# A two-block fp32 network on one core: attention by query tile with both heads at once, ScalarE softmax scaling, real transposes, and a DFT split by output parity

## The chip, the cores and the metric

One core of a Trainium2 chip runs the whole program once. The metric is the device time of that core in microseconds; the median of three runs of the kernel before is 3487.98 us. Engines are named as the profile names them: PE (TensorE, the matmuls), PEld (its weight loads), DVE (VectorE), ACT (ScalarE), POOL (GpSimd) and SP (SyncE, which issues the DMAs).

## What is computed

Two transformer blocks over 512 tokens of width 1024, everything in float32. Cut to the parts that the change touches:

```python
# first block: hybrid_mixer, then memory cross attention, then a mixture of experts
z = h @ w_in                       # aq, ak, av: 8 heads of 64; mu, mv, mo, mi, mf for an mLSTM
y_att = dilated_attention(aq, ak, av)     # causal, three dilated windows, combined by their denominators
y_m   = sigmoid(mo) * (norm(mlstm(...)) + skip * c)
x = x + concat([y_att, y_m]) @ w_out
p = softmax(q @ k.T * Dh**-0.5)           # cross attention: 4 heads, 256 memory keys
x = x + (p @ v) @ w_o

# second block, for each of 2 layers
x = x + 0.5 * swiglu(norm(x), ffn1_w_in[l], ffn1_w_out[l])
q, k, v, uf, ga, gf = split(norm(x) @ mix_w_in[l])
s = q @ k_window.T * Dh**-0.5 + rpb_bias  # neighbourhood attention: 8 rows by 16 columns of an 8 x 64 grid
y_na = softmax(s) @ v_window
y_f  = fft2(uf per group of 128 channels, over (positions, channels)).real
x = x + (sigmoid(ga + b0) * (y_na @ w_na_out) + sigmoid(gf + b1) * (y_f @ w_f_out)) @ w_o
x = x + 0.5 * swiglu(norm(x), ffn2_w_in[l], ffn2_w_out[l])
```

## The kernel before

**Layout.** Activations are feature-major: 128 features on the partitions, 512 tokens along the row. The large products are done in three parts, with each operand split into a high and a low half of type fp32r (`products`, L462 to L464: high x high, low x high, high x low), 8 blocks of 128 features deep, so one call of `gemm` is 24 matmuls of 512 columns. Its weight panel comes by a DMA from SP into `RAW`, ACT rounds it into `WH` (`round_hi`, L855), POOL subtracts (`subtract_lo`, L401) into `WL`, and there are two slots, so a panel is prepared two gemms ahead. DVE takes each result out of `GEMM0`/`GEMM1` (`take`, L1153).

**Order.** All five engines run programs of their own, written by hand; semaphores that count up are the only link. Loops are register loops (`Counts.loop`), and inside one a wait compares a semaphore with a value worked out from the loop register. Stages: memory keys and values; the mixer of the first block, 4 head pairs (a loop of 3 and an unrolled last); output product; cross attention, 2 head pairs, unrolled; router and experts; then a loop over 2 layers with ffn "a", a loop over 4 head pairs ("na"), "comb" and "wo" (gated products), and ffn "b".

**Attention.** One routine on each engine serves the three kinds. It goes through 8 jobs, `jobs = [(h, i) ...]`, first the four query tiles `i` of head 0 of the pair, then those of head 1. For a job PE computes the scores (L533, fp32, 64 rows of the array), DVE adds the bias or the log count (L1180) and reduces the maximum (L1182), ACT takes the exponential and its row sum (L884), DVE inverts the sum (L1188) and multiplies the identity by it (L1189):

```python
chain(v.reciprocal(SMALL[:, 4 + s:5 + s], SMALL[:, 2 + s:3 + s]))
v.tensor_scalar(DIAG[s], IDENT[:, :], SMALL[:, 4 + s:5 + s], None, ALU.mult)
```

PE then transposes and scales in one by an ordinary fp32 matmul with that diagonal (L544), two jobs behind the scores; ACT copies the turned probabilities out of `TURN` into `PT` (L867); and PE multiplies them by the values (L560), three jobs behind the scores, into 64 partitions of `OUT`. An ordinary fp32 matmul stands in the trace as two records, a transpose (`pe.transpose`, L794) as one. Jobs are of 2 key blocks in "na" (192 or 256 keys) and in the cross attention (256 keys), and of 1 to 4 blocks in the mixer.

**The pair in "na".** PE does four gemms (Q, K, V and the Fourier input U), transposes V (L794), does the channel DFT (L801, `CS`: cosine and sine, 256 columns), then the attention with four more gemms (the gates) and the position DFT (L811 and L813: 8 matmuls of 512 columns with `CT` and `NST` into `DEN`) put between its jobs. DVE adds the mask to the two bias tables (L1576) before its first job.

**The mixer pair.** Three gemms, rotation of Q and K (L675, L676), two head products (L683), then the attention with one gemm inside (after the second job's scores), one gemm behind it, and the mLSTM (L692 to L720). ACT does one sigmoid between its exponentials (L902).

## Time and profile before

| | |
|---|---|
| median of 3 runs (lowest, highest) | 3487.98 us (3485.64, 3502.23) |
| profiled execution, span | 3488.2 us |
| PE busy | 3212.4 us (92%), 14634 matmul records |
| DVE busy | 1570.1 us (45%) |
| ACT busy | 773.2 us (22%) |
| POOL busy | 1007.2 us (29%) |
| mean granted TensorE clock | 0.943 |
| mean DMA rate | 94 GB/s |

The profile gives the span from the first to the last instruction of one execution. The profile's page has no other time for that execution; its span lies within the three runs. Busy shares are means over stages with different limits, and a busy PE is not a PE at its peak: the records of consecutive matmuls overlap. A time in the views is the start in us from the beginning of the span, then the duration. PEclk 1.00 is the full clock (2.4 GHz), 0.50 the lower of its two levels (1.2 GHz).

### The profile page before, as it was taken

The numbers are of one execution on the slowest core, as the hardware profiler recorded it, in microseconds if no ns is written. First come the engines' busy times: TensorE is split into PE (matmuls) and PEld (weight loads), VectorE is DVE, ScalarE is ACT, GpSimd is POOL, SyncE is SP. The second block draws the span as 40 slices with busy tenths as digits, with TensorE's granted clock in tenths as the row PEclk, the third lists the DMA queues.
The fourth block names the chain that finished last, engine by engine and source line by source line (L and its number), as shares of the span: only waits on it lengthen the run. The fifth ranks groups of instructions, "written<-read, shape, count | busy, mean of one in ns | idle before, by whom it ended". The sixth has DMA issues, their size and how long they took to land.

```text
span 3488.2 us, 42847 instructions
## 1 busy us (share of the span) xinstructions
PE 3212.4 (92%) x14634; PEld 2520.2 (72%) x14634; DVE 1570.1 (45%) x2036; ACT 773.2 (22%) x1098; POOL 1007.2 (29%) x395
## 2 busy tenths in 40 slices
PE   5888887899999599999998999999999999999997
PEld 4656565678778388877766888888887766678886
DVE  6445575321221542463335642474247333564246
ACT  3233311210100321222223222222222221322121
POOL 2111120100000144442223444444444222344442
PEclk8877887899999799999999999999999999999998
DMA  3110110446646222231212232222222111223232
GB/s 113 43 38 32 38 48 6 160 165 212 210 156 221 97 96 96 96 104 62 68 62 72 85 105 87 96 91 98 94 96 98 63 63 66 66 85 96 97 98 77
DMA packets 87027, 327.43 MB, mean 94 GB/s; under 512 B 9664, under 2 KB 10816, under 8 KB 86336
## 3 DMA queue, kind: packets, MB, share of 16 engines
q1 hardware_dynamic: 86976, 326.76, 28.1%
q8 instruction: 31, 0.51, 0.1%
q14 instruction: 20, 0.16, 0.0%
HBM read 324.63 MB, written 2.10 MB: 94 GB/s over the span
## 4 chain that ended last, share of the span: by engine, by line
issue 56%; PE 26%; POOL 12%; DVE 2%; DMA 1%; POOLq 1%; ACT 1%; DVEq 0%; SPq 0%
POOL WL L401 12%; PE GEMM L462 4%; PE GEMM L463 4%; PE GEMM L464 4%; PE TURN L614 3%; PE SCORE L614 2%; PE GEMM L614 2%; PE GEMM L641 1%; PE DEN L628 1%; DMA E_PANEL<-experts 1%; PE SCORE L600 1%; PE OUT L628 1%; PE TURN L600 1%; POOLq L154 1%; PE TURN L544 1%
## 5 line engine op out<-in xcount | busy, mean ns | idle before, releaser
L401 POOL TENSOR_TENSOR WL<-RAW,WH 128x1024 fp32r<-128x1024 f32 (+1 forms) x379 | 991.5, 2618 | 1866.3 <-ACT WH L855 1866.3
L462 PE MATMUL GEMM<-XH,WH 128*128 128x512 f32 x2152 | 861.0, 400 | 38.6 <-POOL WL L401 32.1
L463 PE MATMUL GEMM<-XL,WH 128*128 128x512 f32 x2152 | 847.9, 394 | 0.0
L464 PE MATMUL GEMM<-XH,WL 128*128 128x512 f32 x2152 | 847.7, 394 | 0.0
L855 ACT CAST WH<-RAW 128x1024 fp32r<-128x1024 f32 (+1 forms) x379 | 416.6, 1103 | 1193.8 <-PE GEMM L464 1178.5
L462 PEld LDWEIGHTS GEMM<-XH,WH 128*128 128x128 f32 x2152 | 410.9, 191 | 149.2 <-issue 52.7
L462 PE MATMUL GEMM<-AH,WH 128*128 128x512 f32 (+1 forms) x1072 | 426.4, 398 | 54.5 <-DVE AL L1164 18.2
L464 PEld LDWEIGHTS GEMM<-XH,WL 128*128 128x128 f32 x2152 | 410.0, 191 | 87.8
L463 PEld LDWEIGHTS GEMM<-XL,WH 128*128 128x128 f32 x2152 | 411.1, 191 | 86.2 <-issue 2.5
L463 PE MATMUL GEMM<-AL,WH 128*128 128x512 f32 (+1 forms) x1072 | 421.4, 393 | 0.0
L464 PE MATMUL GEMM<-AH,WL 128*128 128x512 f32 (+1 forms) x1072 | 421.2, 393 | 0.0
L462 PEld LDWEIGHTS GEMM<-AH,WH 128*128 128x128 f32 x1072 | 206.9, 193 | 110.4 <-issue 24.5
L1163 DVE CAST AH<-PROB 128x512 f32 x104 | 242.2, 2329 | 15.6 <-DVE PROB L1600 2.5
L464 PEld LDWEIGHTS GEMM<-AH,WL 128*128 128x128 f32 x1072 | 206.7, 193 | 42.5
L1153 DVE SCALAR_TENSOR_TENSOR PROB<-GEMM,RS 128x512 f32<-128x512 f32 x88 | 60.9, 692 | 390.8 <-PE GEMM L464 390.8
L463 PEld LDWEIGHTS GEMM<-AL,WH 128*128 128x128 f32 x1072 | 207.2, 193 | 40.7
L1158 DVE SCALAR_TENSOR_TENSOR X<-GEMM,X 128x512 f32 (+1 forms) x96 | 66.4, 692 | 278.9 <-PE GEMM L464 269.1
L417 POOL COPY X<-XN 128x512 f32<-128x512 f32 x4 | 3.5, 885 | 553.8 <-DVE XN L1545 553.8
L544 PEld LDWEIGHTS TURN<-TB,PROB 128*128 128x128 f32 (+1 forms) x480 | 79.6, 229 | 84.6 <-issue 46.2
L544 PE MATMUL TURN<-TB,PROB 128*128 128x128 f32 (+1 forms) x480 | 106.5, 353 | 31.5 <-DVE TB L1189 31.3
L1103 DVE TENSOR_SCALAR XH<-X,VEC (+1 forms) x64 | 126.4, 1976 | 0.0
L897 ACT ACTIVATE TB<-TA 128x512 f32<-128x512 f32 x88 | 55.5, 630 | 260.6 <-DVE TA L1153 260.6
(299 smaller groups left out, 3129.7 us busy)
## 6 DMA issues: line engine op xcount, KB each, us to landing
RAW<-up SPq DMA_DIRECT2D x176, 512.0 KB, 3.3
E_PANEL<-experts SPq DMA_DIRECT2D x128, 512.0 KB, 4.4
RAW<-mix SPq DMA_DIRECT2D x96, 512.0 KB, 3.3
RAW<-down SPq DMA_DIRECT2D x64, 704.0 KB, 4.1
RAW<-experts SPq DMA_DIRECT2D x64, 512.0 KB, 4.4
RAW<-panels SPq DMA_DIRECT2D x43, 512.0 KB, 3.4
AR<-bias SPq DMA_DIRECT2D x16, 320.0 KB, 3.5
X<-xT SPq DMA_DIRECT2D x1, 2048.0 KB, 11.1
```

The lines of the kernel that those rows point to most:

```text
L401: pool.tensor_tensor(WL[slot][:, 0:width], RAW[slot][:, 0:width], f32(WH[slot][:, 0:width]), ALU.subtract).then_inc(split_lo, c.add(split_lo))
L462: pe.matmul(ps, whb, hi, start=(begin and j == 0), stop=False)
L463: pe.matmul(ps, whb, lo, start=False, stop=False)
L464: mm = pe.matmul(ps, wlb, hi, start=False, stop=(end and j == len(blocks) - 1))
L544: mm = pe.matmul(ps[0:size, at * P:(at + 1) * P], PROB[u % 2][:, key - first:key - first + size], DIAG[u % 2], start=True, stop=True)
L600: mm = pe.matmul(bank[:, k * PAIR * P:(k + 1) * PAIR * P], half[:, t * D + d * P:t * D + (d + 1) * P], tile(SEL, t, PAIR * P), start=(t == ...
L614: mm = pe.matmul(ps, tile(E_PANEL[at], k, P), tile(XG, k * PAIR + j, P), start=(k == 0), stop=(k == KD - 1))
L628: mm = pe.matmul(ps[:, :], tile(HID[j], f, P), tile(E_PANEL[at], half), start=(f == 0), stop=(f == FT_MOE - 1))
L855: act.copy(WH[slot][:, 0:width], RAW[slot][:, 0:width]).then_inc(split_hi, c.add(split_hi))
L1103: chain(v.tensor_scalar(hi, x, gain, None, ALU.mult))
L1158: v.scalar_tensor_tensor(x, ps, scale, x, ALU.mult, ALU.add).then_inc(gemm_taken, c.add(gemm_taken))
L1163: chain(v.tensor_copy(hi, src))
```

## The change

- **Jobs.** Attention goes by query tile: the scores of both heads, then the probabilities of both, then the values of both, their matmuls alternating between the heads. There are 4 units instead of 8 jobs. With 2 key blocks the 4 turned blocks of a unit share one `TURN` bank, one copy to `PT` and one signal. `PT` has a new layout, and for the mixer odd units use `TB` and `SQ` for the probabilities.
- **DVE.** One `tensor_tensor_reduce` per head gives minus the logits and their minimum, in place of the sum and the reduction; the built program has it as two instructions, the sum and the reading of its accumulator. One reciprocal serves both heads. The diagonal is gone. The cross attention, which had a plain copy here, now adds a tile of zeros (set once).
- **ACT.** The exponential has scale -1. A new pass per head multiplies the probabilities by the reciprocal (`norms`). In the mixer one weight rounding and the sigmoid move behind the attention.
- **PE.** The transposes are `pe.transpose` with the identity.
- **DFT.** Before the channel DFT, DVE makes the sum and the difference of the two halves of the positions (rows `r` and `r + 4` of the grid) into `SD`; even outputs come from the sum, odd ones from the difference. The position DFT is 8 matmuls of 256 columns. DVE takes its result straight out of `DEN` in a rearranged order.
- **Order in "na".** Written out: three gemms, the first scores, V's transposes, the fourth gemm, and so on. The mask is added to the bias tables before V is taken.
- **Unrolling.** The mixer's loop of 3, the layers and the pairs are Python loops on SP, POOL (layers alone), PE, ACT and DVE; the waits in them compare with constants. The loops inside the ffn, "comb", "wo" and the experts stay. SP waits with a pair's bias DMAs on the scores taken, no longer on the probabilities.

```diff
@@ PE
-            jobs = [(h, i) for h in range(2) for i in range(QT)]
-            def attention(tiles, v, between=None, k_src=KB):
-                for u in range(len(jobs) + 3):
...
-                            mm = pe.matmul(ps[0:size, at * P:(at + 1) * P], PROB[u % 2][:, key - first:key - first + size],
-                                           DIAG[u % 2], start=True, stop=True)
...
+            def turns(tiles, i):
+                first, n = span(tiles[i])
+                blocks = len(tiles[i])
+                together = 2 * blocks <= QT
+                for h in range(2):
+                    pe.wait_ge(probs_ready, c.next(probs_ready))
+                    if h == 0 or not together:
+                        ps, at = turn_bank(), 0
+                    for _, key, size in tiles[i]:
+                        mm = pe.transpose(ps[0:size, at * P:(at + 1) * P], probs(tiles, i, h)[:, key - first:key - first + size], IDENT[:, :])
+                        at += 1
+                    if h == 1 or not together:
                         mm.then_inc(turned_full, c.add(turned_full))
+            def values(tiles, i, v):
+                pe.wait_ge(turned_taken, c.now(turned_taken))
...
+                for n, (at, (place, _, size)) in enumerate(order):
+                    for h in range(2):
+                        from_ = turned_at(tiles)[i][h] + at * P
+                        mm = pe.matmul(OUT[h * HEAD:(h + 1) * HEAD, i * P:(i + 1) * P],
+                                       v[0:size, place * P + h * HEAD:place * P + (h + 1) * HEAD],
+                                       PT[0:size, from_:from_ + P], start=(n == 0), stop=(n == len(order) - 1))
+            def attention(tiles, v, k_src=KB, between=None):
+                scores(tiles, 0, k_src)
+                if between:
+                    between()
+                for i in range(QT):
+                    if i + 1 < QT:
+                        scores(tiles, i + 1, k_src)
+                    if i:
+                        values(tiles, i - 1, v)
+                    turns(tiles, i)
+                values(tiles, QT - 1, v)
...
-                    attention(NEAR, VB, {1: gate, 2: dft, 4: gate, 6: gate, 8: gate})
...
+                    gemm(next_panel(), eight, x_tiles)
+                    scores(NEAR, 1)
+                    turns(NEAR, 0)
+                    pe.wait_ge(halves_ready, c.next(halves_ready))
                     for b in range(2):
                         ps = score_bank()
                         for t in range(2):
                             mm = pe.matmul(ps[:, t * 2 * P:(t + 1) * 2 * P],
-                                           UT[:, (2 * b + t) * P:(2 * b + t + 1) * P], CS[:, :],
+                                           SD[:, (2 * b + t) * P:(2 * b + t + 1) * P], CS[:, :],
                                            start=True, stop=True)
                         mm.then_inc(scores_full, c.add(scores_full))
+                    gemm(next_panel(), eight, x_tiles)
+                    values(NEAR, 0, VB)
+                    scores(NEAR, 2)
+                    turns(NEAR, 1)
...
+                    for b in range(2):
+                        out = DEN[:, b * HALF_T:(b + 1) * HALF_T]
+                        for t in range(2):
+                            at = 2 * b + t
+                            pe.matmul(out, AB[:, at * 2 * P:at * 2 * P + P], tile(CT, at, HALF_T), start=(t == 0), stop=False)
+                            mm = pe.matmul(out, AB[:, at * 2 * P + P:(at + 1) * 2 * P], tile(NST, at, HALF_T),
+                                           start=False, stop=(t == 1))
+                    values(NEAR, 1, VB)
+                    scores(NEAR, 3)
+                    gemm(next_panel(), eight, x_tiles)
+                    turns(NEAR, 2)
+                    gemm(next_panel(), eight, x_tiles)
+                    values(NEAR, 2, VB)
+                    turns(NEAR, 3)
+                    gemm(next_panel(), eight, x_tiles)
+                    values(NEAR, 3, VB)
@@ ACT
+            def norms(tiles, i):
+                act.wait_ge(recips_ready, c.next(recips_ready))
+                for h in range(2):
+                    p = probs(tiles, i, h)
+                    act.activation(p, p, ACT.Copy, scale=stat(2, i, h)).then_inc(probs_ready, c.add(probs_ready))
...
+            def attention(tiles, before=None, between=()):
+                for i in range(QT + 1):
+                    if i < QT:
+                        exps(tiles, i)
+                    if i == 0 and before:
+                        before()
+                    if i:
+                        turned_probs(tiles, i - 1)
+                    if i < QT:
+                        norms(tiles, i)
+                for unit in between:
+                    unit()
@@ DVE
+            def logits(tiles, i, bias):
+                for h in range(2):
+                    p = probs(tiles, i, h)
+                    ps = scores_in()[:, 0:span(tiles[i])[1]]
+                    v.tensor_tensor_reduce(out=p, in0=ps, in1=bias(h, i), scale=-1.0, scalar=-NEG, op0=ALU.add, op1=ALU.min,
+                                           accum_out=stat(0, i, h)).then_inc(scores_taken, c.add(scores_taken))
...
                     take(UT)
+                    v.wait_ge(gemm_taken, c.now(gemm_taken))
+                    near, far = (UT.rearrange("p (c r) -> p c r", r=NA_ROWS)[:, :, r:r + NA_ROWS // 2] for r in (0, NA_ROWS // 2))
+                    for half, op in enumerate((ALU.add, ALU.subtract)):
+                        ins = v.tensor_tensor(tile(SD, half, HALF_T).rearrange("p (c r) -> p c r", r=NA_ROWS // 2), near, far, op)
+                    ins.then_inc(halves_ready, c.add(halves_ready))
@@ all engines
-            with c.loop("mix1", PAIRS - 1):
+            for _ in range(PAIRS - 1):
...
-            with c.loop("layers", LAYERS):
-                with c.loop("na", PAIRS):
+            for l in range(LAYERS):
+                for i in range(PAIRS):
```

Where the instructions stand, in three places. PE in the loop "na" of before, from the end of the position DFT (ISA rows are waits whose value comes from the loop register; `TB` holds the two diagonals):

```order
L540 ISA
L495 ISA
L544 MATMUL TURN<-TB,PROB 64x128
L544 MATMUL TURN<-TB,PROB 128x128
L487 ISA
L533 MATMUL SCORE<-KB,QB 128x192
L540 ISA
L495 ISA
L544 MATMUL TURN<-TB,PROB 128x128 x2
L549 ISA
L556 ISA
L560 MATMUL OUT<-PT,VB 64x128 x2
```

PE in the changed kernel, a pair of "na", between the fourth gemm and the fifth (`BIG` holds `SD` there):

```order
L549 MATMUL SCORE<-KB,QB 128x256 x2
L562 MATMUL TURN<-IDENT,PROB 64x128
L562 MATMUL TURN<-IDENT,PROB 128x128
L562 MATMUL TURN<-IDENT,PROB 64x128
L562 MATMUL TURN<-IDENT,PROB 128x128
L837 MATMUL SCORE<-CS,BIG 128x256 x4
```

The rows of waits are gone, scores come in twos and turns in fours, and the channel DFT stands behind the first unit's turns. On DVE, the changed kernel from the mask to the two halves (`AR` holds the bias tables, `PADU` is U):

```order
L1658 TENSOR_TENSOR AR<-AR 128x640 x2
L1234 SCALAR_TENSOR_TENSOR VT<-GEMM,RS 128x512
L1252 ISA PROB,SMALL<-SCORE,AR 128x192
L1252 ISA SMALL 128x1
L1252 ISA PROB,SMALL<-SCORE,AR 128x192
L1252 ISA SMALL 128x1
L1258 RECIPROCAL SMALL<-SMALL 128x2
L1234 SCALAR_TENSOR_TENSOR PADU<-GEMM,RS 128x512
L1667 TENSOR_TENSOR BIG<-PADU 128x256 x2
```

Before, the two mask additions stood behind U and the copies of the channel DFT, and nothing stood between the taking of U and PE's channel DFT.

## Rows read from the trace of the kernel before

**Rows 1.** The page: busy time by engine, and the granted clock in 40 slices.

```profile
PE 3212.4 (92%) x14634; PEld 2520.2 (72%) x14634; DVE 1570.1 (45%) x2036; ACT 773.2 (22%) x1098; POOL 1007.2 (29%) x395
...
PEclk8877887899999799999999999999999999999998
```

**Rows 2.** Windows: us, busy by engine, PEclk, DMA: mixer, cross, layers' pairs.

```profile
188.32:280.44 92.12, 81.10 (x288) 55.29 (x287) 47.98 (x74) 27.78 (x48) 14.41 (x6) 0.80 0.11 36
...
509.00:543.00 34.00, 31.81 (x104) 21.90 (x104) 12.15 (x36) 7.79 (x24) 0.36 (x1) 0.60 0.04 16
...
1647.47:1719.27 71.80, 69.32 (x302) 50.16 (x301) 24.91 (x49) 16.04 (x34) 19.63 (x8) 1.00 0.21 68
...
2780.15:2855.08 74.93, 72.44 (x302) 52.23 (x301) 24.89 (x50) 16.04 (x35) 19.58 (x8) 0.95 0.19 65
```

**Rows 3.** Timeline, DVE: the pair's first two takes.

```profile
1647.47 0.69 DVE L1153 SCALAR_TENSOR_TENSOR QB<-GEMM,RS 128x512 f32<-128x512 f32 x1 [4.04 <-PE GEMM L464]
1652.91 0.69 DVE L1153 SCALAR_TENSOR_TENSOR KB<-GEMM,RS 128x512 f32<-128x512 f32 x1 [4.75 <-PE GEMM L464]
```

**Rows 4.** Timeline, PE, the same pair: transposes, position DFT, small groups.

```profile
1663.60 0.71 PE L794 MATMUL TURN<-IDENT,VT 128*128 128x128 f32 x5
...
1674.54 1.13 PE L811 MATMUL DEN<-BIG,AR 128*128 128x512 f32 x2
...
1681.60 0.85 PE L544 MATMUL TURN<-TB,PROB 128*64 128x128 f32 x4
...
1684.06 0.71 PE L544 MATMUL TURN<-TB,PROB 128*128 128x128 f32 x4 [1.09 <-DVE TB L1189]
1684.69 0.79 PE L560 MATMUL OUT<-PT,VB 128*64 128x128 f32 x4
1685.42 0.59 PE L533 MATMUL SCORE<-KB,QB 64*128 64x192 f32 x2
```

**Rows 5.** Timeline, PE, 1712.0 to 1712.1: two column halves of the array.

```profile
1712.04 0.27 PE L544 MATMUL TURN<-TB,PROB 128*64 128x128 f32 x1
1712.05 0.27 PE L560 MATMUL OUT<-PT,VB 128*64 128x128 f32 x1
```

**Rows 6.** Waits of PE in the pair 1647.47:1719.27.

```profile
PE TURN L544 <- DVE TB L1189: 1.5, 3, 1.1
```

**Rows 7.** Timeline in the ffn: DVE and POOL at one moment.

```profile
1524.85 3.51 DVE L1103 TENSOR_SCALAR XH<-X,VEC  x1
1524.85 3.22 POOL L401 TENSOR_TENSOR WL<-RAW,WH 128x1408 fp32r<-128x1408 f32 x1 [4.26 <-ACT WH L855]
```

**Rows 8.** Timeline of the pair: POOL at a panel, DVE's mask additions.

```profile
1648.60 2.39 POOL L401 TENSOR_TENSOR WL<-RAW,WH 128x1024 fp32r<-128x1024 f32 x1 [5.65 <-ACT WH L855]
...
1667.29 4.53 DVE L1576 TENSOR_TENSOR AR<-AR 128x640 f32<-128x640 f32 x2
```

**Rows 9.** Waits of PE in the mixer pair 188.32:280.44.

```profile
PE TURN L544 <- DVE TB L1189: 3.3, 3, 1.4
```

**Rows 10.** Timeline, a looped mixer pair, PE: its attention's ends and turns.

```profile
202.53 3.10 PE L533 MATMUL SCORE<-KB,QB 64*128 64x128 f32 x6 [2.75 <-DVE AR L1329]
...
237.46 2.08 PE L544 MATMUL TURN<-TB,PROB 128*128 128x128 f32 x8
...
241.71 0.50 PE L462 MATMUL GEMM<-XH,WH 128*128 128x512 f32 x1
```

**Rows 11.** The unrolled last mixer pair: first scores, and OUT taken by DVE.

```profile
386.13 2.26 PE L533 MATMUL SCORE<-KB,QB 64*128 64x128 f32 x6 [2.46 <-DVE AR L1329]
...
422.71 0.69 DVE L1195 CAST AH<-OUT 128x512 fp32r<-128x512 f32 x1 [5.92 <-PE OUT L560]
```

**Rows 12.** PE groups of the cross attention, 509:577, with idle before.

```profile
L544 PE MATMUL TURN<-TB,PROB 128*128 128x128 f32 x64 | 19.0, 451 | 2.9 <-DVE TB L1189 2.9
...
L462 PE MATMUL GEMM<-AH,WH 128*128 128x512 f32 x5 | 2.7, 542 | 2.8 <-issue 2.8
```

**Rows 13.** DMA queues of the whole program: packets, MB, share.

```profile
q8 instruction: 31, 0.51, 0.1%
```

265 lines of the change are left out of this document (140 added, 125 removed).

## The prediction

> **What bounds the kernel now.** I read the page first: PE is busy in 92% of the span, and the slices where its clock is low are the first seven and a few at the layers' transitions [rows 1]. Then the windows by stage. A mixer pair takes 92.12 us at a mean granted clock of 0.80, a cross attention pair 34.00 us at 0.60, a pair of "na" 71.80 us at 1.00 in the first layer and 74.93 us at 0.95 in the second [rows 2]. In all of them PE works nearly throughout and DVE, ACT and POOL less than 60% of the time, so what PE is given decides, and only waits that PE itself shows count beside it. In "na" those are small: 1.5 us for the diagonals [rows 6], some 2.3 us with the smaller ones. The eight gemms of a pair take 5.44 us each (the distance of two takes, [rows 3]), 43.5 us, and the change leaves them. What is left to change is 71.8 - 43.5 = 28.3 us a pair, 26.0 us of it work of PE: fp32 matmuls of a few blocks. That, eight times, and the attention stretches of the four mixer pairs and two cross pairs are all the change can reach, about 8 x 28 + 4 x 32 + 2 x 27 = 406 us.
>
> **"na", a pair.** *Position DFT.* It runs from 1674.54 to the turn at 1681.60 [rows 4], 7.06 us for 8 matmuls of 512 columns. With 256 columns each: half, **-3.5**. The channel DFT stays at four matmuls.
>
> *Turns.* A group of two turned blocks takes 0.63 us up to the next group (1684.06 to 1684.69), 8 groups are 5.0 us. A real transpose costs (0.71 - 0.27) / 4 = 0.11 us by the five of V, whose one record lasts about 0.27 us [rows 4, 5]. Four groups of four with 0.2 us to start each: 4 x 0.64 = 2.6 us, **-2.4**.
>
> *Values.* A group is 0.73 us (1684.69 to 1685.42, [rows 4]), 8 are 5.8 us. Now a group holds both heads, alternating, each writing its own 64 partitions. If they follow each other, 4 x 1.2 = 4.8; if two matmuls that fill different column halves run at once, 4 x 0.8 = 3.2. The trace has one such pair by chance: a turn of 64 columns and a values matmul of the other head start 0.01 us apart and last 0.27 us each [rows 5]. I take the overlap, **-2.6**; the other end is -1.0.
>
> *Scores.* The two heads use different row halves; before, two jobs that followed each other used the same one. No row shows row halves at once. One scores group takes about 0.5 us up to the gemm behind it, 8 are 4.0 us; at once it is -2.0, one after the other -0.4 (fewer groups). I take **-1.3**.
>
> *Waits.* The wait for the diagonal goes: **-1.5** [rows 6]. The scaling pass on ACT (two of about 0.4 us) lies under a gemm of 5.44 us for units 0, 1 and 3, and for unit 2 between other work; I cost it at nothing, and about 0.5 us a unit if that cover is gone. The tensor_tensor_reduce costs DVE between 0.36 us (the sum alone) and 0.75 us (sum and reduction as now); DVE is at 24.9 of 71.8 us [rows 2] and it is hidden either way.
>
> *A new wait.* PE's channel DFT now waits for the two halves. Behind the fourth gemm PE has the second scores and the first turns, about 1.2 us. DVE has to take U (0.69 us) and make the halves (twice about 0.42 us), about 1.7 us: PE would stand 0.5 us. But ACT rounds a panel at the same release as DVE takes a result, and POOL follows 1.13 us after that take, for 2.39 us [rows 3, 8]. That is while the first half is being made. The trace shows what then happens: POOL and a DVE operation from SBUF to SBUF start at the same 1524.85, POOL takes its 3.22 us and the DVE operation, which alone is under 0.5 us, lasts 3.51 [rows 7]; and the two mask additions, beside two POOL operations, take 4.53 us together [rows 8]. So the second half is ready about 2.4 us later and PE stands 2.9 us. Both ends kept, I take **+2.0**. The Trainium skill, *SBUF — State Buffer* (section "SBUF: two separate sides"), says that DVE and GpSimd hold a shared port pair exclusively for a whole instruction, also when a DVE operation has two SBUF inputs; by that rule the term is +2.9, and the rows agree with it.
>
> Sum: -3.5 - 2.4 - 2.6 - 1.3 - 1.5 + 2.0 = **-9.3** a pair, **-75** for eight. The ends are -5 (no overlap, the whole new wait) and -13.
>
> **Mixer, a pair.** The attention runs from 202.53 to the gemm at 241.71, 39.2 us with one gemm in it [rows 10], and mostly at the low clock. Turns: 40 records at (2.08 - 0.39) / 7 = 0.24 us [rows 10] are 9.7 us; 20 transposes at twice 0.11 are 4.4: -5.3. Values of both heads at once: 40 records, at most the turns' 0.24, so half of 9.7, less 0.5 for the starts, -4.3. Scores: -2 of some 8 us (the first three jobs' six records take 3.10, [rows 10]). PE's waits for the diagonals, of which the longest stands behind the sigmoid's table load that now lies behind the attention: -3.3 [rows 9]. New: values wait for the copy of the very turns before them (on DVE's and ACT's chain of sum, exponential, reciprocal, scaling, copy), some 1.2 us a unit, less the scores that stand in between: +4. Waits with constants: the unrolled last pair needs at most 422.71 - 386.13 = 36.6 us [rows 11] against 39.2, so -1 a pair beyond the rest. Sum -11.9; as the chain may hold PE longer when it has less to do I take **-11**, **-44** for four; ends -5 and -16.
>
> **Cross attention, both pairs.** 64 turn records at 0.24 become 32 transposes at 0.22: -8.3. Values at once -4, scores -3, the waits of 2.9 us [rows 12] -2.9, the longer chain within a unit +3. **-15**, ends -6 and -24.
>
> **Unrolling.** Elsewhere it removes only register instructions beside PE's work: 0. The DMAs of a pair keep their order on SP; the bias DMAs wait for scores, which are taken no later than the old signal, some three gemms ahead of their use: 0. The other moved steps (a weight rounding behind the mixer's attention, its gemm a gemm later; the output taken from `DEN` directly) are off PE's path.
>
> **The sum.** -75 - 44 - 15 = -134 us against the profiled span of 3488.2 us, which is 0.2 us from the median of the runs: **3354 us**.
>
> **The rivals.** *The clock.* The clock falls where PE does small fp32 work: in the second layer's pairs it is lost after the position DFT and costs 74.93 - 71.80 = 3.1 us a pair; the first layer's same stretch keeps it [rows 2]. The change makes a new thin stretch, transposes and then the wait before the channel DFT. If every pair loses the clock there, and the second layer's keep their present loss, that is 8 x 3.1 = 25 us; with the overlaps absent too (1.6 + 0.9 us a pair, 3 us in a mixer or cross pair) 25 + 20 + 18 = 63: **3417**. For it: the first layer is as dense as the second. Against: the stretch of 12 us without a gemm around the DFT becomes about 7. The Trainium skill, *TensorE: Matmul & The Clock Gate* ("Part 4: PE-mode transpose"), says that transposes do not count as PE activity for the clock; that makes this rival likelier, and no row separates it from fp32 work. Chance 0.22.
>
> *Everything overlaps.* Scores too, the halves are made before POOL gets in, and the shorter stretches leave the clock up in the second layer and in half of the mixer's stretch: 8 x -12 - 3.1 x 4 - 4 x 16 - 22 = -194: **3294**. Chance 0.15.
>
> *The straight code has to be fetched.* The trace has 31 instruction packets of 0.51 MB, 16 KB each [rows 13], with the loops; PE's program now has 4501 rows for 2067, so some 35 fetches more. PE has one idle of 2.8 us by "issue" alone, in straight code [rows 12]. At 2.8 us each it would be +98 us, no slower than before; it turns slower from 134 / 35 = 3.8 us a fetch, and at 4.5 us, one and a half times the gap seen, it is +158: **3512**. Against it: the unrolled last mixer pair is faster than the looped ones [rows 11], and those 2.8 us are the only such gap. Chance 0.05.
>
> *PE is not the bound that it seems:* the chain DVE, ACT, PE, ACT of a unit, with its two more steps, holds PE for as long as the turns and values are shortened in mixer and cross attention, and in "na" every unit's probabilities come late by 1 us. Then only the DFT's 3.5, less the new wait of 2.0, stays: 8 x -1.5 = -12: **3476**, no change. For it: the last third of the mixer's attention has no gemm to hide behind. Against: those links are 0.3 to 0.7 us and PE has 2 to 4 us of work beside them. Chance 0.05.
>
> **The numbers.** Chances: forecast 0.53, clock 0.22, everything overlaps 0.15, fetch 0.05, chain 0.05. The range takes in the ends of the terms and the first two rivals but not the last two: 3285 to 3430. A measurement of this kernel tells 0.5% (17 us) from no change. Faster: the first three, 0.90, less 0.01 for their upper tail; same: 0.05 of the chain and 0.01; slower: the fetch, 0.05.
>
> **What would show it.** Right: pairs of "na" at 60 to 65 us, PE standing 0.5 to 3 us before the channel DFT with DVE's second half 2.4 us long, position DFT at 3.5 us, values of the two heads starting 0.01 us apart, mixer pairs near 81 us and cross pairs near 26. Wrong: idle by "issue" on PE at equal distances in the unrolled parts; a low clock in every pair of "na" in gemms behind the channel DFT; values at 0.11 us from start to start with no pairs; PE waiting for ACT's scaled probabilities over 1 us in most units.

## The result, and the profile after

| | before | after |
|---|---|---|
| median (lowest to highest) | 3492.82 us (3485.64 to 3502.23, 4 runs) | 3275.09 us (3269.72 to 3276.82, 4 runs) |
| ratio, 95% interval | | 0.9376 [0.9350, 0.9401] |
| span of the profiled execution | 3488.2 us | 3274.2 us |
| mean granted TensorE clock | 0.943 | 0.960 |

Faster, as forecast, but by 214 us of span where the forecast was 134, and 10 us below the lower end of the range. Below, *turns* are the matmuls or transposes that turn the probabilities (L544, now L562), *values* those that multiply them by the values (L560, now L576), and the *clock* is the granted clock of TensorE as a share of the full one. The page of the changed kernel, busy time, granted clock and instruction packets (against [rows 1] and [rows 13]):

```profile
PE 3012.9 (92%) x14394; PEld 2408.0 (74%) x14394; DVE 1467.6 (45%) x1877; ACT 799.2 (24%) x1156; POOL 1008.8 (31%) x395
...
PEclk8899887999999799999999999999999999999998
...
q8 instruction: 46, 0.75, 0.1%
```

The windows (us, busy by engine, PEclk, DMA share, GB/s) of a looped mixer pair, a cross pair, and a pair of "na" in each layer, against [rows 2]:

```profile
167.58:242.21 74.63, 63.98 (x268) 43.25 (x267) 40.23 (x63) 28.81 (x54) 15.04 (x7) 0.91 0.15 44
...
440.72:461.12 20.40, 17.28 (x88) 11.11 (x88) 5.84 (x24) 9.71 (x28) 0.00 (x0) 0.75 0.08 27
...
1604.12:1662.76 58.64, 57.42 (x287) 45.03 (x286) 17.17 (x39) 18.59 (x39) 19.41 (x8) 1.00 0.26 83
...
2616.98:2675.61 58.63, 57.41 (x287) 45.02 (x286) 17.16 (x39) 18.58 (x39) 19.41 (x8) 1.00 0.25 84
```

The mixer pair fell from 92.1 to 74.6 us and its clock rose from 0.80 to 0.91; the cross pair fell from 34.0 to 20.4 us with the clock up from 0.60 to 0.75; a pair of "na" fell from 71.8 and 74.9 us to 58.6 in both layers. The layer's last pair, up to the taking of its output, has the full clock too:

```profile
1662.76:1715.66 52.90, 51.64 (x261) 40.18 (x259) 15.78 (x36) 18.20 (x38) 17.01 (x7) 1.00 0.22 71
```

By stage: the mixers from their first take of Q to that of the cross attention, the other two from their first take of Q to the taking of the last pair's attention output (`AH`):

| stage | before | after | gain | forecast |
|---|---|---|---|---|
| four mixer pairs and the output product | 415.7 | 348.1 | 67.6 | 44 |
| two cross pairs | 60.1 | 34.8 | 25.3 | 15 |
| eight pairs of "na" | 281.7 + 294.2 | 228.8 + 228.8 | 118.3 | 75 |
| everything else | | | 2.8 | 0 |

The timeline of the "na" pair, DVE's first two takes and PE's work from the third gate on (against [rows 3] and [rows 4]):

```profile
1604.12 0.69 DVE L1234 SCALAR_TENSOR_TENSOR QB<-GEMM,RS 128x512 f32<-128x512 f32 x1 [4.31 <-PE GEMM L485]
1609.49 0.69 DVE L1234 SCALAR_TENSOR_TENSOR KB<-GEMM,RS 128x512 f32<-128x512 f32 x1 [4.68 <-PE GEMM L485]
...
1631.43 0.81 PE L576 MATMUL OUT<-PT,VB 128*64 128x128 f32 x8
1632.16 0.70 PE L549 MATMUL SCORE<-KB,QB 64*128 64x256 f32 x4
1632.80 0.65 PE L562 MATMUL TURN<-IDENT,PROB 128*128 128x128 f32 x4
1633.29 0.60 PE L852 MATMUL DEN<-BIG,AR 128*128 128x256 f32 x2
...
1636.84 0.66 PE L576 MATMUL OUT<-PT,VB 128*64 128x128 f32 x8
```

The distance of two takes is 5.37 us (it was 5.44). The position DFT takes 3.55 us, from 1633.29 to 1636.84 (it was 7.06). A group now holds both heads: eight records of values in 0.66 to 0.81 us, where a group of four took 0.73, four transposes in 0.65, and the scores of both heads in 0.70. The same by groups: PE's lines in one pair before (1647.47:1719.27) and, below, after (1545.50:1604.12). Columns: line, engine, operation, names, shapes, count, busy us, mean ns, idle before.

```profile
L544 PE MATMUL TURN<-TB,PROB 128*128 128x128 f32 x24 | 4.6, 300 | 1.5 <-DVE TB L1189 1.5
L560 PE MATMUL OUT<-PT,VB 128*64 128x128 f32 x24 | 4.3, 287 | 0.2 <-ACT PT L867 0.2
...
L533 PE MATMUL SCORE<-KB,QB 64*128 64x256 f32 x8 | 2.8, 428 | 0.3 <-DVE AR L1572 0.3
L533 PE MATMUL SCORE<-KB,QB 64*128 64x192 f32 x8 | 2.4, 375 | 0.0
...
L544 PE MATMUL TURN<-TB,PROB 128*64 128x128 f32 x8 | 1.7, 298 | 0.0
L560 PE MATMUL OUT<-PT,VB 64*64 64x128 f32 x8 | 1.7, 294 | 0.0
```

```profile
L562 PE MATMUL TURN<-IDENT,PROB 128*128 128x128 f32 x12 | 2.3, 282 | 0.0
L576 PE MATMUL OUT<-PT,VB 128*64 128x128 f32 x24 | 2.2, 289 | 0.0
L837 PE MATMUL SCORE<-CS,BIG 128*128 128x256 f32 x8 | 2.0, 388 | 0.9 <-DVE SMALL L1252 0.9
L549 PE MATMUL SCORE<-KB,QB 64*128 64x256 f32 x8 | 1.4, 428 | 0.0
L549 PE MATMUL SCORE<-KB,QB 64*128 64x192 f32 x8 | 1.2, 375 | 0.0
L562 PE MATMUL TURN<-IDENT,PROB 128*64 128x128 f32 x4 | 1.0, 279 | 0.0
L576 PE MATMUL OUT<-PT,VB 64*64 64x128 f32 x8 | 0.9, 294 | 0.0
```

PE's busy time counts overlapping records once, so halves of the array that run at once show as a shorter busy time with the same mean. Turns went from 6.3 to 3.3 us, values from 6.0 to 3.1, scores from 5.2 to 2.6, the DFT by 3.5, and PE's idle from 2.5 to 1.2: 3.0 + 2.9 + 2.6 + 3.5 + 1.3 = 13.3, the 13.2 us gained but for rounding.

PE's waits in the mixer pair 167.58:242.21 (engine, line, what it waited for: us in total, times, longest), against [rows 9]:

```profile
PE SCORE L715 <- DVE TA L1405: 2.8, 1, 2.8
PE OUT L576 <- ACT PT L910: 2.5, 3, 1.6
```

The wait for the diagonals (3.3 us) is gone, and the new one for the copy of the turned blocks has 2.5 us of it back. Nearly the whole gain of this pair lies in the stretch from the attention's first scores to the gemm behind it, which took 39.18 us at a clock of 0.61 before (202.53 to 241.71):

```profile
L544 PE MATMUL TURN<-TB,PROB 128*128 128x128 f32 x40 | 10.6, 426 | 3.4 <-DVE TB L1189 3.3
L533 PE MATMUL SCORE<-KB,QB 64*128 64x128 f32 (+3 forms) x16 | 9.5, 702 | 2.9 <-DVE AR L1329 2.7
L560 PE MATMUL OUT<-PT,VB 128*64 128x128 f32 x40 | 9.2, 391 | 0.0
```

and takes 21.57 us at 0.84 after it (184.52 to 206.09):

```profile
L549 PE MATMUL SCORE<-KB,QB 64*128 64x128 f32 (+3 forms) x16 | 4.4, 507 | 1.0 <-DVE AR L1413 0.9
...
L576 PE MATMUL OUT<-PT,VB 128*64 128x128 f32 x40 | 3.1, 283 | 2.6 <-ACT PT L910 2.5
L562 PE MATMUL TURN<-IDENT,PROB 128*128 128x128 f32 x8 | 1.4, 293 | 0.0
L562 PE MATMUL TURN<-IDENT,TB 128*128 128x128 f32 x6 | 1.1, 291 | 0.0
```

### The profile page after: what moved, and what is told of

It reads as the page before. It is cut to its first block, busy times and chain, and to the rows that moved or that the text cites. A ratio compares the mean times of both kernels' runs of the same rounds, so it can differ in the third digit from the quotient of the medians.

```text
span 3274.2 us, 40376 instructions
## 1 busy us (share of the span) xinstructions
PE 3012.9 (92%) x14394; PEld 2408.0 (74%) x14394; DVE 1467.6 (45%) x1877; ACT 799.2 (24%) x1156; POOL 1008.8 (31%) x395
## 4 chain that ended last, share of the span: by engine, by line
issue 62%; PE 18%; POOL 15%; DVE 2%; DMA 1%; ACT 1%; POOLq 1%; DVEq 0%; SPq 0%
POOL WL L422 15%; PE TURN L646 3%; PE SCORE L646 3%; PE GEMM L646 2%; PE GEMM L673 1%; PE SCORE L632 1%; PE DEN L660 1%; DMA E_PANEL<-experts 1%; PE GEMM L483 1%; PE OUT L660 1%; PE GEMM L485 1%; PE GEMM L484 1%; PE TURN L632 1%; PE GEMM L623 0%; POOLq L163 0%
## 5 line engine op out<-in xcount | busy, mean ns | idle before, releaser
L1234 DVE SCALAR_TENSOR_TENSOR PROB<-GEMM,RS 128x512 f32<-128x512 f32 x88 | 60.9, 692 | 398.0 <-PE GEMM L485 397.9
L1234 DVE SCALAR_TENSOR_TENSOR TA<-GEMM,RS 128x512 f32<-128x512 f32 x92 | 63.7, 692 | 100.1 <-PE GEMM L485 98.8
L1245 DVE TENSOR_TENSOR AL<-PROB,AH 128x512 f32 x104 | 72.1, 693 | 12.8
```

Of the source, the lines that this page charges most:

```text
L1234: v.scalar_tensor_tensor(dst, ps, scale, by, ALU.mult, ALU.mult).then_inc(gemm_taken, c.add(gemm_taken))
L1245: v.tensor_tensor(lo, src, f32(hi), ALU.subtract).then_inc(operand_ready, c.add(operand_ready))
```

## The experiments

Each kernel is the changed kernel with one edit, unless it says otherwise. "na" is the length of a pair, "mixer" the three looped pairs, each with its mean granted clock. "Measured" gives the difference to the changed kernel's 3275.09 us; the kernel before, measured beside each of them, stood at 3488 to 3490 us.

| kernel | median us (range, runs) | ratio to before, 95% | na | mixer pairs (clock) | cross pair (clock) |
|---|---|---|---|---|---|
| before | 3488 to 3493 | 1 | 71.8, 74.9 | 94.6, 92.1, 91.8 (.84 .80 .80) | 33.8 (.60) |
| after | 3275.09 | 0.9376 [0.9350, 0.9401] | 58.6 | 74.9, 74.6, 74.0 (.91 .91 .91) | 20.4 (.75) |
| 1 before, loops written out | 3464.82 (3458.97 to 3475.51, 8) | 0.9929 [0.9903, 0.9955] | 71.4, 71.4 | 88.3, 91.6, 90.8 (.86 .80 .79) | 33.0 (.60) |
| 2 turns by matmul | 3297.66 (3293.62 to 3298.63, 4) | 0.9446 [0.9401, 0.9492] | 60.8 | 76.0, 75.2, 75.1 (.91 .91 .91) | 22.4 (.77) |
| 3 values apart | 3284.96 (3283.10 to 3287.51, 4) | 0.9416 [0.9371, 0.9460] | 60.1 | 75.9, 74.8, 75.0 (.91 .91 .91) | 20.4 (.75) |
| 4 only transposes | 3367.66 (3358.87 to 3371.51, 4) | 0.9644 [0.9595, 0.9692] | 65.3 | 83.0, 81.6, 81.5 (.84 .83 .83) | 27.8 (.57) |
| 5 scores parted | 3330.85 (3320.58 to 3336.38, 4) | 0.9538 [0.9518, 0.9558] | 60.4 | 82.9, 82.0, 83.0 (.81 .81 .82) | 27.8 (.57) |
| 6 single column between | 3330.36 (3329.16 to 3334.53, 4) | 0.9545 [0.9531, 0.9560] | 60.9 | 82.6, 81.3, 76.3 (.83 .83 .91) | 28.3 (.58) |
| 7 DFT twice | 3299.84 (3296.73 to 3309.30, 4) | 0.9463 [0.9442, 0.9483] | 62.1 | 75.0, 72.5, 74.2 (.91 .93 .91) | 20.0 (.77) |
| 8 gemm ahead of the DFT | 3267.61 (3265.19 to 3272.22, 5) | 0.9369 [0.9355, 0.9383] | 57.7 | 75.3, 74.8, 74.2 (.91 .91 .91) | 20.4 (.75) |
| 9 single column, gemm within | 3332.94 (3326.65 to 3336.67, 4) | 0.9556 [0.9541, 0.9571] | 60.9 | 83.6, 82.5, 78.5 (.86 .86 .89) | 28.5 (.58) |
| 10 before again | 3488.11 (one run) | | 71.8, 74.9 | 95.1, 91.8, 91.9 (.82 .80 .80) | 33.0 (.60) |
| 11 after again | 3274.97 (3273.49 to 3280.01, 5) | 0.9389 [0.9376, 0.9402] | 58.6 | 75.2, 74.7, 74.0 (.91 .91 .91) | 20.4 (.75) |
| 12 the eighth again | 3268.07 (3264.76 to 3271.30, 5) | 0.9368 [0.9355, 0.9380] | 57.7 | 75.2, 73.5, 73.6 (.91 .93 .91) | 20.4 (.75) |
| 13 both heads from the same rows | 3286.91 (3281.33 to 3289.54, 4) | 0.9424 [0.9408, 0.9440] | 59.4 | 74.9, 72.9, 73.7 (.91 .93 .91) | 25.3 (.60) |
| 14 matmul turns, all apart | 3367.00 (3361.90 to 3373.07, 4) | 0.9647 [0.9627, 0.9668] | 64.7 | 79.0, 78.5, 86.1 (.91 .91 .82) | 31.6 (.57) |

**1. The loops of the kernel before written out** (of layers, "na" pairs and mixer pairs, on each engine).

```diff
-                with c.loop("na", PAIRS):
+                for i in range(PAIRS):
```

> The kernel before, with the loops over layers, pairs of na and mixer pairs written out, and nothing else. Theory 1 (the clock: the part of the gain that I did not forecast comes from the clock that the shorter attention stretches keep): writing out is worth at most 1 us a mixer pair, 3480 to 3490 us, and the mixer stretch stays near a mean clock of 0.80. Theory 2 (waits with constants instead of waits with registers): the distance of two gemms in na falls from 5.44 to 5.37 us (0.07 x 64 = 4 us), the looped mixer pairs fall towards the last one (3 x 2.6 = 8 us), the small groups gain some 0.05 us each (64 groups in na, 8 us): 3465 to 3470 us. If most of the unforecast 80 us were of this kind it would be 3410.

Measured: -25 us against the kernel before beside it (3489.87). The windows of a mixer pair and of a pair of "na" in the first and in the second layer:

```profile
181.06:272.70 91.64, 81.20 (x288) 55.68 (x287) 47.32 (x75) 26.48 (x48) 14.73 (x7) 0.80 0.12 36
...
1646.10:1717.50 71.40, 69.33 (x303) 50.15 (x302) 25.00 (x49) 16.01 (x35) 19.60 (x8) 1.00 0.23 69
...
2769.69:2841.10 71.41, 69.34 (x303) 50.17 (x302) 25.01 (x49) 16.03 (x35) 19.60 (x8) 1.00 0.23 68
```

The time is theory 2's, but by luck: its sum is not what the windows show. The distance of two gemms is 5.37 us, as it said, but that is 0.4 us a pair; the first mixer pair gains 6.3 us with its clock up from 0.84 to 0.86, the two others 0.5 to 1.0, and the unrolled last one loses 2.5. The largest part is the second layer, where the pairs keep the clock: 4 x 3.5 = 14 us. But the last pair of the first layer, which had the full clock in the loop, now loses it for a while, some 38 us into the pair:

```profile
1828.00:1830.00 2.00, 2.00 (x6) 1.53 (x5) 1.93 (x4) 0.00 (x0) 0.69 (x1) 0.50 0.09 14
```

It takes 67.3 us up to the taking of its output where the looped kernel took 66.3. So writing out, which I had costed at nothing in "na", came with the full clock in seven pairs of eight in place of four; why, the records don't say, and that it would do so each time is not shown.

**2. The probabilities turned by an ordinary matmul.**

```diff
-                        mm = pe.transpose(ps[0:size, ...], probs(tiles, i, h)[...], IDENT[:, :])
+                        mm = pe.matmul(ps[0:size, ...], probs(tiles, i, h)[...], IDENT[:, :], start=True, stop=True)
```

> The changed kernel, with the probabilities turned by ordinary fp32 matmuls with the identity in place of transposes; everything else, the scaling on ACT too, as changed. At the full clock a turn of 128 x 128 should cost about 0.1 us more (20 a pair of na, 20 a mixer pair, 32 in cross attention: 272 x 0.1 = 27 us): 3302 us. Theory 1 (the clock hangs on how much fp32 work stands between gemms): the mixer's attention falls back to the low clock, and the time is 3330 to 3350. Theory 2 (the clock is kept for another reason): 3295 to 3305 with the mixer's stretch as in the changed kernel.

Measured: +22.6 us, theory 2. A pair of "na" costs 2.13 us more (20 x 0.11), a mixer pair 0.5 to 1.1, and the mixers' clock stays at 0.91: the kind of instruction does not decide the clock here. The Trainium skill (*TensorE: Matmul & The Clock Gate*, "Part 4: PE-mode transpose") says that a transpose does not count as a busy PE in the same way for the clock; here "na" with transposes is granted 1.00 throughout, and the mixers' clock is the same with and without them, so no cost of that kind shows.

**3. The values head after head.**

```diff
-                for n, (at, (place, _, size)) in enumerate(order):
-                    for h in range(2):
+                for h in range(2):
+                    for n, (at, (place, _, size)) in enumerate(order):
```

> The changed kernel, with the values matmuls of one head behind those of the other, so that no two that follow each other fill different column halves. If the halves of the changed kernel run at once, 10 matmul pairs a pair of na and of mixer, 16 a cross pair... cost 0.2 us each more: 8 x 2 + 4 x 2 + 6 = 30 us, 3305 us at the same clock; if they don't, 3275. If the longer stretches lose the clock in the mixers and cross attention, 3320 to 3340.

Measured: +10 us, a third of what I expected. In "na" 1.43 us a pair (values busy 4.8 us, in place of 3.1): the column halves do overlap. In the cross pair nothing, in the mixers at most 1: there PE waits for ACT's copy anyway.

**4. Without overlaps and shorter DFT** (the edits of 3, 5 and 7 together).

> The changed kernel without its overlaps and without the shorter DFT: values head after head, the two heads' scores parted by other work, and every matmul of the position DFT issued twice (the second pass overwrites the first, with the same result). What stays of the change is the real transpose with the scaling on ACT, and the unrolling. Sum of the parts at a kept clock: values +30, scores 4 x 0.4 a pair, +20, DFT +28: 3353 us. Theory 1 (the clock hangs on the length of the fp32 stretch): more than the sum, 3380 to 3410, with a mean clock below 0.9 in the mixer's stretch. Theory 2 (transposes alone keep the clock): the sum, and a mixer stretch at 0.9 or more.

Measured: +92.6 us. In "na" the sum holds: 58.63 + 1.43 (values) + 1.81 (scores, by 5) + 3.46 (DFT, by 7) = 65.33, and 65.33 was measured. In the mixers 7 to 8 us a pair are lost with the clock at 0.83. The whole, 3367.7 us, lies between the sum (3353) and theory 1's 3380 to 3410; the clock below 0.9 is theory 1's, but its reason, the length of the stretch, is not borne out by 9 and 14.

**5. The scores of the two heads parted** by other work.

```diff
-                        scores(tiles, i + 1, k_src)
+                        scores(tiles, i + 1, k_src, heads=(0,))
                     if i:
                         values(tiles, i - 1, v)
+                    if i and i + 1 < QT:
+                        scores(tiles, i + 1, k_src, heads=(1,))
```

> The changed kernel with the scores of the two heads parted: head 1's matmul of a query tile stands behind other work of PE (the values or turns of another tile, once the turns of V), so no two that follow each other use different row halves. By the runs so far a pair of na with scores parted, values apart and the DFT doubled lost 6.7 us, of which values alone 1.4; if the DFT is 3.5, the scores are 1.8 us a pair (14 us in all). In mixer and cross attention the parted run lost 7 us a pair, values alone 0.3 and 0: theory 1 (it is the parting of the scores that costs it there, by overlap, by a later head 1 in the chain, and by the clock that falls with it) expects 7 us a mixer pair and 7 a cross pair again, with a mean clock below 0.87 in the mixers: 3275 + 14 + 28 + 14 = 3331. Theory 2 (only values and scores together lose the clock) expects 2 to 3 us a pair there: 3300.

Measured: +55.8 us, 8 x 1.8 in "na", 7.4 to 9.0 a looped mixer pair, 7.4 the first cross pair: theory 1's number.

**6. A matmul of one column between the two heads' scores.**

```diff
+                    if h == 1:
+                        pe.matmul(ps[:, 0:1], IDENT[:, :], ONES[:, 0:1], start=True, stop=True)
```

> The changed kernel with one matmul of a single column, over all 128 rows and columns, between the scores of head 0 and head 1 of each query tile; it writes the first column of head 1's bank, which head 1's scores then overwrite. The order of all else is kept, so the two heads' scores can't run at once but neither comes later for another reason. If the overlap of row halves is what the parted scores lose: about 1.8 us a pair of na plus 4 x 0.05 for the extra matmuls, 3275 + 16 + (mixer and cross pairs at 2 to 3 us, if the clock holds) 15 = 3306; with the clock lost in the mixers as in the parted run, 3325 or more. If the parted runs lose by their order alone, 3280.

Measured: +55.3 us, as with the scores parted, and the case in which the mixers lose the clock. But the three mixer pairs, which run the same instructions, did not do the same:

```profile
178.51:259.76 81.25, 72.17 (x276) 48.10 (x275) 40.52 (x63) 29.68 (x54) 15.26 (x7) 0.83 0.14 41
259.76:336.02 76.26, 66.76 (x276) 44.53 (x275) 40.33 (x62) 29.26 (x54) 14.79 (x7) 0.91 0.14 44
```

In windows of 2 us the granted clock falls at three places in the first of them and at two in the other; the extra one begins some 30 us into the pair, inside the attention, and lasts 14 us. It costs 5.0 us.

**7. The position DFT issued twice.**

```diff
-                    for b in range(2):
+                    for b in (0, 1, 0, 1):
```

> The changed kernel with every matmul of the position DFT issued twice, 16 of 256 columns a pair, as many columns as before the split; the second pass overwrites the first with the same result. If the DFT's PE time is on the path and nothing else hangs on it: +3.5 us a pair, 3275 + 28 = 3303, all of it in the eight pairs of na, clock 1.00. If the DFT is what lost the clock in the second layer before, its pairs lose 3 us more each: 3315.

Measured: +24.8 us, 3.46 a pair at a clock of 1.00. The DFT is fully on the path, and doubling it loses no clock.

**8. The fifth gemm ahead of the channel DFT.** In the changed kernel PE's only wait of weight in a pair of "na" stands there. The timeline:

```profile
1622.09 0.69 DVE L1234 SCALAR_TENSOR_TENSOR PADU<-GEMM,RS 128x512 f32<-128x512 f32 x1 [3.97 <-PE GEMM L485]
...
1622.82 0.76 DVE L1667 TENSOR_TENSOR BIG<-PADU 128x256 f32<-128x256 f32 x2
1623.20 2.60 POOL L422 TENSOR_TENSOR WL<-RAW,WH 128x1024 fp32r<-128x1024 f32 x1 [4.69 <-ACT WH L898]
1623.49 0.42 DVE L1252 CUSTOM_DVE_ANT_0 PROB<-SCORE,AR 128x256 f32<-128x256 f32 x1
...
1624.07 1.97 PE L837 MATMUL SCORE<-CS,BIG 128*128 128x256 f32 x8 [0.89 <-DVE SMALL L1252]
```

PE has been idle since 1623.18. The halves are ready at 1623.58, 0.40 us on. PE starts 0.49 us later still, when DVE has also taken the second tile's first scores (the logits at 1623.49) out of the bank that the DFT wants. The edit puts a gemm over both, and moves the orders of DVE and ACT accordingly:

```diff
                     turns(NEAR, 0)
+                    gemm(next_panel(), eight, x_tiles)
                     pe.wait_ge(halves_ready, c.next(halves_ready))
...
-                    gemm(next_panel(), eight, x_tiles)
                     values(NEAR, 0, VB)
-                    scores(NEAR, 2)
                     turns(NEAR, 1)
+                    scores(NEAR, 2)
+                    gemm(next_panel(), eight, x_tiles)
```

> The changed kernel with the order of a pair of na changed: the fifth gemm stands ahead of the channel DFT in place of behind it, the sixth between the channel and the position DFT, and DVE's and ACT's orders follow (PE's wait for the two halves then has 5.4 us of gemm ahead of it, and the copies of the DFT's first result have the sixth gemm over them). Theory 1 (the 0.9 us that PE waits for the halves is the only stall there): -0.9 x 8 = -7 us, 3268. Theory 2 (the fetching and turning chain of the probabilities takes the wait over, because the values of a tile now stand closer behind its copy): no change, 3275, with new waits of PE for ACT's PT.

Measured: 57.74 us a pair in place of 58.63, and of PE's two waits in a pair, 0.9 and 0.3 us, the second is left:

```profile
PE TURN L827 <- DVE VT L1234: 0.3, 1, 0.3
```

Theory 1.

**9. The single column again, and a gemm moved into the mixer's attention.**

```diff
+                    if within and i == 2:
+                        within()
                     turns(tiles, i)
```

> The kernel with the single-column matmul between the heads' scores (3330 us; two of its looped mixer pairs at 82 us and a clock of 0.83, one at 76 us and 0.91), and in the first three mixer pairs the gemm that follows the attention moved inside it, between the values of the second query tile and the turns of the third. PE's work is the same; the longest stretch without a gemm is halved. Theory 1 (the clock falls because PE has done small fp32 work without a gemm for too long, and the low clock then costs 5 to 6 us): all looped mixer pairs at 0.88 or more; they take 76 us plus up to 3 us for the wait that the moved gemm no longer covers at the attention's end, 3315 to 3328 in all. Theory 2 (the low clock has another cause, or the fence itself): pairs of 82 us or more at 0.83, 3330 to 3340.

Measured: no gain, 3332.94 us. In the second pair the clock fell at 208 us, 3 us after the attention's first gemm and before the moved one (216 us), during which it came back; the pair's mean is 0.86 in place of 0.83, and a wait at the attention's end that grew from 1.3 to 3.8 us took that gain. Theory 1 fails: a stretch of 3 us of small matmuls behind a gemm was enough, so its length is not what decides.

**10, 11, 12. Both kernels again, and the eighth beside the changed one.**

> The kernel before, unchanged, profiled once more. Writing out its loops seemed to bring 25 us, of which the profile puts 14 us on the second layer's pairs, which kept the clock (71.4 in place of 74.9 us). Theory 1 (the looped code loses the clock there each time): 74.9 us and 0.95 again. Theory 2 (it varies from execution to execution): 71.8 us and 1.00, and a span near 3475 us.

> The changed kernel, unchanged, beside the reordered one on the same chip: 3275 us, a pair of na at 58.64 us.

> The kernel with the fifth gemm ahead of the channel DFT once more, beside the changed kernel on the same chip. If the 0.9 us of waiting for the halves is saved in each pair: 57.74 against 58.64 us, 7 us less in the whole, 0.2%.

The kernel before shows the same clock at the same places: theory 1. Beside the changed kernel on one chip the reordered one is 6.9 us faster (3268.07 against 3274.97), with no run of the one within the range of the other; the pairs account for 8 x 0.9 = 7.2. It is the fastest kernel of this study.

**13. Both heads' scores from the same 64 rows.** Order and number of instructions are the changed kernel's; the kernel leaves out head 1's own scores, so that part of its output is not the network's.

```diff
-                    part = slice(h * HEAD, (h + 1) * HEAD)
+                    part = slice(0, HEAD)
```

> The changed kernel with head 1's scores taken from the same 64 rows of QB and KB as head 0's (so the second head's attention is computed from the first head's scores: that part of the output is not the reference's). Order and number of instructions are the changed kernel's; only the row halves can no longer run at once. Theory 1 (the parted and the fenced scores lost 55 us by the overlap and the clock that goes with it): 3320 to 3330, mixer pairs at 80 us or more with a mean clock near 0.83, cross pairs at 27 to 28 us, na pairs at 60.4. Theory 2 (they lost it by the added or moved instructions): 3275 to 3290.

Measured: +12 us, theory 2 (3286.91). PE's scores groups in a pair of "na", the same shapes as above with 1.4 and 1.2 us, and the cross pair:

```profile
L549 PE MATMUL SCORE<-KB,QB 64*128 64x256 f32 x8 | 2.3, 402 | 0.0
L549 PE MATMUL SCORE<-KB,QB 64*128 64x192 f32 x8 | 1.8, 348 | 0.0
```

```profile
439.38:464.72 25.34, 23.06 (x88) 15.32 (x88) 6.09 (x24) 10.13 (x28) 0.00 (x0) 0.60 0.07 21
```

The overlap of the row halves is real, 1.5 us of PE in a pair of "na" (0.8 on its path, since the waits of 0.9 and 0.3 shrink to one of 0.5) and 4.9 us in a cross pair, where the clock falls with it. In the mixers it is worth nothing: they keep 0.91 to 0.93 and their 73 to 75 us. So 5 and 6 did not lose their 7 to 9 us there by the overlap alone: in 6 the clock is 5.0 of it, and the pair that kept it (76.3 us) is 2.2 us above the changed kernel's 74.0. In 5 no pair kept the clock, so there the split is not measured.

**14. Matmul turns, scores parted and values apart together.**

> The changed kernel with the scores parted, the values head after head and the probabilities turned by ordinary fp32 matmuls: of the change, the scaling on ACT without the diagonals, both heads' turns in one group, the shorter DFT and the unrolling stay. In na the sum should hold: 58.63 + 2.13 + 1.43 + 1.81 = 64.0 us a pair. In the mixers the run with parted scores and values apart took 81.6 us at a clock of 0.83, and matmul turns alone cost 0.7 us there at 0.91. Theory 1 (with the clock low PE's work is the bound of the mixer's attention, so the turns cost their full price): +4 us or more, 85 to 87 us, and cross pairs at 31; 3368 - 28 + 17 + 16 + 7 = 3380. Theory 2 (a chain over DVE and ACT is the bound there): +1 us, 82.5 us; 3362.

Measured: 3367.00 us. In "na" 64.7 (64.0 by the sum). The mixers:

```profile
174.70:253.18 78.48, 67.98 (x288) 46.74 (x287) 40.02 (x62) 29.26 (x54) 14.81 (x7) 0.91 0.14 42
253.18:339.23 86.05, 75.62 (x288) 51.56 (x287) 40.27 (x63) 29.62 (x54) 14.83 (x7) 0.82 0.13 39
```

Two of the three pairs kept the clock, with more small fp32 work than 5, which lost it in all three. Neither theory had that. The same instructions take 78.5 us with the clock and 86.1 without: 7.6 us. The pair without the clock costs 3 to 4.5 us more than in 4 and 5, about what 20 turns cost at half the clock (20 x 0.22 = 4.4, an estimate from 2), and 78.5 is 4 more than the changed kernel.

## Why the prediction was wrong

The direction was right and the mechanisms were named, but nearly all sizes fell on one side. The 80 us that were missed are 43 in "na", 24 in the mixers, 10 in cross attention and 3 elsewhere. Four steps failed:

1. the clock of the mixer's and the cross attention, kept as it was, with no term in the sum: it rose from 0.80 to 0.91 and from 0.60 to 0.75, and in the same instructions it is worth 5.0 to 7.6 us a mixer pair (6, 14);
2. the second layer's lost clock, kept: it came back, 12.5 us;
3. the new wait before the channel DFT, +2.0 us a pair: 0.9;
4. the overlap of the scores, -1.3 us a pair: -2.6.

Term by term, for a pair (numbers in brackets are the experiments):

- **Position DFT, -3.5: right** (3.46 by experiment 7). **Turns, -2.4:** 3.0 by PE's busy time; the kind of instruction alone is 2.13 (2), the rest I put down to fewer groups, which no run isolates. **Values, -2.6:** 2.9, of which the overlap is 1.43 on the path (3).
- **Scores, -1.3: too small.** I took half of the possible overlap because no row showed row halves at once, and PE spends 2.6 us less. I had counted a group as 0.5 us up to the gemm behind it; its busy time is 0.65 (5.2 / 8), and two heads in a group take no more than one (0.60 to 0.70).
- **The waits, -1.5 + 2.0: the wrong sign of the sum.** PE's idle fell by 1.3 us, where I had it grow by 0.5. The step that failed is POOL's part in the new wait. That PE would stand some 0.5 us for the halves was right (0.40); the other 0.49 of the 0.9 us is for the scores' bank (8), which I had not seen. But I had POOL get between the two halves and hold the second for 2.4 us. The second began 0.04 us before POOL came and lasts 0.42 us, not 2.4 (rows below).
- **Gemms unchanged: not quite.** 5.37 us for 5.44. The written-out kernel before has the same 5.37, and its pair is 0.4 us shorter (1), all of it in PE's idle.
- **The second layer's lost clock, kept in the forecast: wrong.** 4 x 3.1 = 12.5 us. I had it as a part of the rival "everything overlaps". The kernel before with its loops written out gets it back as well (1), and I had costed that at nothing in "na"; it lost the clock once in another pair, which the changed kernel does in none.
- **Mixer pair, -11: 17.5 to 19.7 in the looped ones, 12.7 in the unrolled last.** Pairs that lost the clock stand at 81.5 to 83 us in 4 and 5, 9 to 12 us below the looped ones before, so the work was about right as far as these runs tell. On top of it comes the clock, which is worth 5.0 (6) to 7.6 us (14) in the same instructions. No run has the changed kernel's own instructions at the low clock, so the split for that kernel is not measured. I had read the low clock in the attention [rows 10] as a property of the work left in it. Before, it fell 28 us into the pair and stayed low for 24 us; in the changed kernel that fall is gone. Two are left in the pair, each behind waits of PE: at 185 us behind the rotation (2.8 us) and at 215 us behind the gates' rows. The term for the chain, +4, showed as 2.5 us of waiting for the copy.
- **Cross pair, -7.5: 13.4 in the first.** By PE's busy time turns fell from 9.8 to 3.6 us, values from 8.7 to 3.3, scores from 8.9 to 5.2, and its idle grew by 1.3. Undone one at a time, the row halves give 4.9 (13) with the clock up from 0.60 to 0.75, the transposes 2.0 (2), the overlap of the values 0 (3); the other 6.5 us no run isolates.
- **Unrolling elsewhere, 0, and no stall for code:** 46 instruction packets for 31, not 66, and 2.8 us everywhere else. PE's idle by "issue" behind the cross attention is 2.8 us as before. The rival of the fetches had nothing in it.

The rows of the new wait in the changed kernel:

```profile
1623.16 0.42 DVE L1667 TENSOR_TENSOR BIG<-PADU 128x256 f32<-128x256 f32 x1
```

```profile
1623.20 2.60 POOL L422 TENSOR_TENSOR WL<-RAW,WH 128x1024 fp32r<-128x1024 f32 x1 [4.69 <-ACT WH L898]
```

My own numbers said as much: 0.69 + 0.42 = 1.11 us from the take of U to the end of the first half, and POOL 1.13 us behind that take. The mask additions of the same pair show the other order, POOL from 1610.68 and the second addition behind it:

```profile
1610.95 2.90 DVE L1658 TENSOR_TENSOR AR<-AR 128x640 f32<-128x640 f32 x1
```

The Trainium skill (*SBUF — State Buffer*, "SBUF: two separate sides") says that of the two engines the one that starts first keeps the shared ports for its whole instruction, and that the other is blocked. In both places the rows agree on who is held. On the amount they agree only in part: POOL would lose 0.38 us to the second half (1623.20 to 1623.58), and its operation lasts 2.60 us where the one at 1616.11 lasts 2.40. My step had the order of arrival wrong, not the rule.

Two sums of the prediction are off, without effect on the forecast: the ends of a pair of "na" add up to -5.9 and -12.0, where it has -5 and -13.

The rival that the clock is lost in every pair of "na" is refuted: 1.00 in all eight, even with the DFT doubled or matmul turns. The rival nearest to the truth is "everything overlaps", 3294 us, whose clock terms were still too small: it gave the clock back in half of the mixer's stretch, where the long fall went altogether. I had given it 0.15. The forecast took the overlap of the values in full and that of the scores at half, and let no clock come back; the range ended 9 us below this rival, and not at the full overlap with the clock regained.

**What stays open:** why the clock falls inside the mixer's attention or doesn't. It falls at one place, some 30 us into the pair, or not at all. It is not the transposes (2), not the overlap of scores or values (3, 13), not the amount of small fp32 work (14 against 5), and not the length of the stretch behind a gemm (9); in 6 and 14 the same instructions did both in one execution. All three pairs of the kernel before lost it, none of the changed kernel's. That the parted and fenced scores lose 55 us, and sharing rows only 12, is therefore measured and its cause is not shown. That the changed kernel owes its clock in the mixers to the change is shown by its two profiles against two of the kernel before and by 1, where the written-out loops alone leave 0.79 and 0.80 in the second and third pair; which part of the change does it is not shown. Nor did I try the changed kernel with its loops kept.

## What to carry to other kernels

Where a stage shows a granted clock well below the others, price the change twice, with that clock kept and with it regained, and let both into the range: here the clock alone was 5 to 8 us of a pair of 76 to 86. Before a term lets one engine hold another, add up the two arrival times from the rows: a few hundredths of a us in the order decided 2.4 us here. And when parts of a change are undone one at a time, undo one also without adding or moving an instruction: parted and fenced scores agreed to 1 us, and both seemed to price the overlap where most of the loss in the mixers was the clock.

## What the runs showed of the hardware

- Two fp32 matmuls of 64 rows in different row halves run at once: four records of 256 columns take 0.70 us, and 1.13 from the same rows (both at the full clock, in the mixers at 194 us). Eight records of values for both heads, in column halves, take 0.66 to 0.81 us.
- `tensor_tensor_reduce` shows as a record of 0.42 us and one of 0.08 for 256 columns; sum and reduction as two instructions took 6.2 us for the eight jobs of a pair of "na", now eight records take 2.8 us and their accumulator reads 0.7.
- With the loops written out, so that waits compare with constants in place of registers, the distance of two gemms of 24 matmuls is 5.37 us for 5.44 (1).
- Two DVE operations with both inputs in SBUF followed each other 0.34 us apart (records of 0.42 us); POOL, coming 0.04 us after the second's start, took 2.60 us for 2.40. Where POOL came before the second one's start, that one took 2.90 us.
- Equal instructions can run at two clocks in successive passes of one execution, a mixer pair at 76.3 and 81.3 us, or 78.5 and 86.1.
